# Preparing the first two units of a feed-forward on VectorE and ScalarE instead of GpSimd

## Chip, cores and metric

The kernel runs on one core of a Trainium2 chip. The metric is the device time of one execution in microseconds (us), the median of three runs. A time within a trace is given in us from the start of its span.

## What is computed

One inference step of a decoder layer for 1,088 tokens (1,024 of a prompt, 64 of samples) with a model width of 1,024: feed-forward a, a mixer (a state-space scan beside sparse attention), an attention over memory, feed-forward b, a final norm. The change touches both feed-forwards and nothing else. Each of them is, in float32:

```python
def rmsnorm(x, g):
    xf = x.astype(jnp.float32)
    xf = xf * lax.rsqrt(jnp.mean(xf * xf, axis=-1, keepdims=True) + EPS)
    return (xf * g.astype(jnp.float32)).astype(x.dtype)

def swiglu_ffn(x, g, w_in, w_out):
    h = rmsnorm(x, g) @ w_in
    gate, up = jnp.split(h, 2, axis=-1)
    return (jax.nn.silu(gate) * up) @ w_out        # D_FF = 2816
```

## The kernel before

`ffn_stage` is called twice, at the program's start ("first feed-forward") and at its end ("second", from 2093.7 us). Its product of x with the gate and up weights is done as 2x2 blocks with seven products instead of eight (M1 to M7): five are of a sum or difference of blocks on one side or both. A float32 factor is split in two parts, high (ScalarE rounds it, `round_w` L555 and `round_h` L573) and low (VectorE subtracts the high part, `rest_w` L820 and `rest_h` L815), and each product is three matmuls (L674 to L676).

A unit is one tile of gate and up outputs by one half of the tokens; there are 44. For the first two units, u = 0 and 1, the operands of x must first be made. That goes in eight blocks j = 0 to 7 (`PREPS`), four for each unit: block j is 272 columns by two pairs of the 128-row tiles of x. For a block:

- `scale(j)`, VectorE, L807 to L809: x times the norm's weights, two instructions of 128x272 and one of 128x544. It also fills one of two buffers `b12`, and waits until block j - 2 has been turned.
- `turn(j)`, GpSimd, L513 to L518: four differences T1 to T4 of 128x272. T2 needs T1, and T4 needs T2.
- `round_h(j)`, ScalarE, then `rest_h(j)`, VectorE: both parts of all seven operands, one instruction of 128x1904 each.
- TensorE: seven products, 21 matmuls of 272 columns.
- In the first feed-forward alone also `square(j)` on ScalarE (L566, two of 128x544) and 16 matmuls of 136 columns (L687), which sum the squares for the norm. The second has them from the stage before it.

The weights of the first tile arrive as four blocks. `combine(0)`, GpSimd, L525 to L533, makes five sums of 128x512, each from parts that `rest_w` has let go of (the order is fixed by the semaphores `w_ready` and `s_made`). Later tiles have their sums made on VectorE already, in its own `combine(f, n)`.

After block 3, `first_unit(0)` (L851 to L866) adds the products of unit 0 on VectorE. In the first feed-forward a ScalarE root (`root`, L580, with a table load) must come before three of these adds and before the fourth block's TensorE products from M2 on. After block 7 comes `invert(0)` (L901, a reciprocal of 3.55 us), then the gate of unit 0, `first_unit(1)`, and from `invert(1)` on the loop over units 2 to 43. Every engine works its list in the written order:

```python
                scale(0)
                scale(1)
                for a in (A11, A12):
                    rest_w(0, a)
                rest_h(0)
                for a in (S1, S3, S2, S4, A22):
                    rest_w(0, a)
                for j in range(1, PREPS):
                    if j + 1 < PREPS:
                        scale(j + 1)
                    rest_h(j)
```

## Time and profile before

| | |
|---|---|
| median of 3 runs | 2914.68 us (2910.53 to 2921.82) |
| the profiled execution, its own time | 2912.39 us |
| its span | 2910.7 us |
| TensorE busy | 2671.4 us, 92% |
| VectorE, ScalarE, GpSimd busy | 1589.0, 986.7, 222.8 us |
| first feed-forward, 0 to 80 us: TensorE, VectorE, GpSimd busy | 46.87, 55.84, 45.57 us |
| second, 2115 to 2170 us: TensorE, VectorE, GpSimd busy | 33.22, 45.14, 28.28 us |

The profiled execution lies 2.3 us under the median of the runs. Busy time says who works; the chain of waits and the timelines say who is waited for. Two instructions of one engine overlap a little in the records, so that the distance between two starts, not the duration of one, is what an instruction costs in a queue.

### The profile page before, as it was taken

How to read it: one execution, taken by the hardware profiler on the slowest of the kernel's cores; microseconds unless marked ns; L12 is line 12 of the kernel's file. 1: busy time of each engine (PE TensorE's matmuls, PEld its weight loads, DVE VectorE, ACT ScalarE, POOL GpSimd, SP SyncE). 2: the span in 40 equal slices, each digit the busy share in tenths (PEclk: the TensorE clock that was granted, in tenths of full speed). 3: DMA queues.
4: the chain of work that ended last, by engine and by line, in shares of the span. 5: the costliest groups of instructions: out<-in, count | busy, mean ns of one | idle time of the engine just before them, and what ended most of it. 6: DMA issues, size and time to landing. Idle time of an engine off the chain costs nothing. (4 is left out here: it accounts for less than half of the span.)

```text
span 2910.7 us, 47240 instructions
## 1 busy us (share of the span) xinstructions
PE 2671.4 (92%) x18982; PEld 2506.4 (86%) x18982; DVE 1589.0 (55%) x2870; ACT 986.7 (34%) x2080; POOL 222.8 (8%) x248
## 2 busy tenths in 40 slices
PE   6899999999979998999589997797769999999998
PEld 5899999999969997898467774697669999999997
DVE  6766666544264111343477663565586666665434
ACT  4333333311144222221266662343433333332111
POOL 6000000000000000110200004030440000000000
PEclk9999999999989998998699997798879999999999
DMA  2222222512035324130300005203012222232121
GB/s 96 71 85 69 78 79 71 191 75 75 1 137 107 40 75 168 39 99 5 101 23 23 8 1 190 119 11 104 16 37 78 79 71 86 68 132 107 75 75 62
DMA packets 121995, 220.29 MB, mean 76 GB/s; under 512 B 12834, under 2 KB 76754, under 8 KB 120242
## 3 DMA queue, kind: packets, MB, share of 16 engines
q1 hardware_dynamic: 115922, 201.51, 21.6%
q10 hardware_dynamic: 2880, 9.07, 0.8%
q0 software_dynamic: 2976, 6.68, 0.7%
q8 instruction: 152, 2.49, 0.4%
q14 instruction: 65, 0.53, 0.1%
HBM read 170.80 MB, written 48.24 MB: 75 GB/s over the span
## 5 line engine op out<-in xcount | busy, mean ns | idle before, releaser
L674 PE MATMUL ffn_gate_up<-ffn_h_hi,ffn_w 128*128 128x272 f32 x1912 | 560.0, 293 | 60.7 <-DVE ffn_h_lo L815 42.6
L675 PE MATMUL ffn_gate_up<-ffn_h_lo,ffn_w 128*128 128x272 f32 x1912 | 557.5, 292 | 0.0
L676 PE MATMUL ffn_gate_up<-ffn_h_hi,ffn_w 128*128 128x272 f32 x1912 | 556.7, 291 | 0.0
L674 PEld LDWEIGHTS ffn_gate_up<-ffn_h_hi,ffn_w 128*128 128x128 f32 x1912 | 364.8, 191 | 66.2 <-DVE ffn_h_lo L815 32.5
L676 PEld LDWEIGHTS ffn_gate_up<-ffn_h_hi,ffn_w 128*128 128x128 f32 x1912 | 364.7, 191 | 0.0
L675 PEld LDWEIGHTS ffn_gate_up<-ffn_h_lo,ffn_w 128*128 128x128 f32 x1912 | 364.6, 191 | 0.0
L1007 DVE SCALAR_TENSOR_TENSOR x<-ffn_down,x 128x364 f32<-128x364 f32 (+1 forms) x240 | 126.3, 534 | 327.7 <-PE ffn_down L235 327.7
L820 DVE TENSOR_TENSOR ffn_w<-ffn_w_raw,ffn_w 128x512 fp32r<-128x512 f32 x264 | 187.8, 714 | 102.7 <-ACT ffn_w L555 102.7
L555 ACT ACTIVATE ffn_w<-ffn_w_raw 128x512 fp32r<-128x512 f32 x264 | 159.9, 624 | 97.3 <-PE ffn_down L676 79.1
L674 PE MATMUL ffn_down<-ffn_h_hi,ffn_w 128*128 128x272 f32 x552 | 163.6, 296 | 13.4 <-DVE ffn_w L820 7.9
L233 PE MATMUL mix_ps<-h_mix_hi,mix_w_hi 128*128 128x364 f32 x480 | 161.0, 335 | 9.3 <-issue 6.1
L675 PE MATMUL ffn_down<-ffn_h_lo,ffn_w 128*128 128x272 f32 x552 | 162.1, 294 | 0.0
L676 PE MATMUL ffn_down<-ffn_h_hi,ffn_w 128*128 128x272 f32 x552 | 161.9, 293 | 0.0
L234 PE MATMUL mix_ps<-h_mix_lo,mix_w_hi 128*128 128x364 f32 x480 | 160.0, 333 | 0.0
L235 PE MATMUL mix_ps<-h_mix_hi,mix_w_lo 128*128 128x364 f32 x480 | 159.8, 333 | 0.0
L1929 DVE TENSOR_TENSOR mix_w_lo<-mix_w_raw,mix_w_hi 128x1024 fp32r<-128x1024 f32 (+1 forms) x26 | 32.1, 1233 | 196.5 <-ACT mix_w_hi L1814 196.5
L1295 PE MATMUL ssd_hid_ps<-ssd_pages,ssd_cmp_w 128*128 128x128 f32 (+1 forms) x1024 | 138.8, 294 | 0.0
L2394 DVE TENSOR_REDUCE pn_neg_max<-pn_s_ps 128x1 f32<-128x640 f32 (+7 forms) x128 | 90.4, 707 | 88.2 <-PE pn_s_ps L2221 49.1
L1295 PEld LDWEIGHTS ssd_hid_ps<-ssd_pages,ssd_cmp_w 128*128 128x128 f32 x1024 | 131.7, 193 | 2.4
L651 ACT ACTIVATE ffn_h_hi<-ffn_h_raw 128x1088 fp32r<-128x1088 f32 x44 | 48.7, 1107 | 232.1 <-DMA ffn_h_raw<-scratch_ffn_act 232.0
L586 ACT ACTIVATE ffn_sums<-ffn_sums 128x544 f32<-128x544 f32 x88 | 58.0, 659 | 201.9 <-DVE ffn_sums L873 201.8
L233 PE MATMUL ffn_down<-ffn_h_hi 128*128 128x364 f32 (+1 forms) x384 | 126.2, 329 | 0.0
(520 smaller groups left out, 6506.2 us busy)
## 6 DMA issues: line engine op xcount, KB each, us to landing
ffn_w_raw<-in_w_ffn_in SPq DMA_DIRECT2D x88, 512.0 KB, 3.9
scratch_ffn_act<-ffn_prod SPq DMA_DIRECT2D x88, 272.0 KB, 2.6
ffn_h_raw<-scratch_ffn_act SPq DMA_DIRECT2D x44, 544.0 KB, 7.0
mix_w_raw<-in_w_mix SPq DMA_DIRECT2D x20, 512.0 KB, 3.5
ffn_h_raw<-in_w_ffn_out SPq DMA_DIRECT2D x16, 512.0 KB, 9.2
ssd_pages<-in_cmp_pages SPq DMA_DIRECT2D x64, 128.0 KB, 2.1
ffn_w_sum<-in_w_ffn_out SPq DMA_DIRECT2D x14, 512.0 KB, 11.1
scratch_x<-x SPq DMA_DIRECT2D x1, 4368.0 KB, 16.7
```

Of the source, the lines that this page charges most:

```text
L233: pe.matmul(out, w_hi, x_hi, start=start, stop=False)
L234: pe.matmul(out, w_hi, x_lo, start=False, stop=False)
L235: return pe.matmul(out, w_lo, x_hi, start=False, stop=stop)
L555: act.activation(w[:, a, 0, :], fresh(a), ACT.Copy).then_inc(w_hi_ready, 1)
L586: act.activation(gate_view(u), gate_view(u), ACT.Silu).then_inc(gate_done, 1)
L674: pe.matmul(out, hi, x_hi, start=start, stop=False, skip_group_check=chained)
L675: pe.matmul(out, hi, x_lo, start=False, stop=False, skip_group_check=chained)
L676: mm = pe.matmul(out, lo, x_hi, start=False, stop=stop, skip_group_check=chained)
L820: dve.tensor_tensor(w[:, a, 1, :], fresh(a), w[:, a, 0, :].bitcast(F32), ALU.subtract).then_inc(w_ready, 1)
L1007: dve.scalar_tensor_tensor(xT[:, t, cols], dn_bank(d), 0.5, xT[:, t, cols], ALU.mult, ALU.add).then_inc(dn_added, 1)
L1295: mm = pe.matmul(hp[j % 2][:, 1 - later:1 - later + w].rearrange("p (b n) -> p b n", n=PAGES), w1s[:, kv, k, hh * P:(hh + 1) * P], pages[: ...
L2394: m = dve.tensor_reduce(neg_max[:, u % 2, 0:1], s[:, 0:w], AX_X, ALU.max, negate=True)
```

## The change

GpSimd keeps only a memset. Its `turn` goes to VectorE for all eight blocks, and so does its `combine(0)`, now interleaved one by one with the `rest_w` of the first tile. `scale(j)` stays on VectorE for j = 0 and 1 and goes to ScalarE for j = 2 to 7 (`OWN_SCALES = 2`), as three copies with a scale read from memory. ScalarE rounds block 0 before all weights, and `square(j)` comes one block later in its queue. The load of the norm's weights is put ahead of the first block of x.

```diff
--- before.py
+++ after.py
@@ -265,6 +265,7 @@
 UPPER_BANKS_FIRST = ("M5", "M6", "M7", "M1", "M2", "M4", "M3")
 WIDTHS = (TG, TG, HALVES * HALF - 2 * TG)
 DOWN_CHUNKS = (2, 5, 5, 5, 5)
+OWN_SCALES = 2
 
 
 def in_two_types(nc, stack, name, shape):
@@ -502,42 +503,11 @@
                 if fin is not None:
                     fin.stores(sp)
 
-            @block.gpsimd
-            def _(pool):
-                def turn(j):
...
-                    pool.wait_ge(scaled_x, j + 1)
-                    pool.tensor_tensor(at_(T1), extra, at_(B11), ALU.subtract).then_inc(turned, 1)
...
-                def combine(f):
...
-                if first_loads is not None:
                     pool.memset(xT[:, :, HALVES * HALF:], 0.0).then_inc(pads_ready, 1)
-                turn(0)
-                combine(0)
-                for j in range(1, PREPS):
-                    turn(j)
+            if first_loads is not None:
+                @block.gpsimd
+                def _(pool):
+
             def fresh(a):
 
                 return {A11: raw[:, 0], A12: raw[:, 1], S2: w_raw[:, S2, 1, :], S1: raw[:, 2], S3: raw[:, 0],
@@ -565,6 +535,19 @@
                             act.wait_ge(sq_summed, j)
                         act.activation(out, x_block(xT, j)[:, n], ACT.Square).then_inc(sq_ready, 1)
 
+                def scale(j):
+
+                    g, kp = divmod(j, K_PAIRS)
+                    if arrivals is not None:
+                        act.wait_ge(arrivals[j], 32)
+                    act.wait_ge(turned, 4 * max(j - 1, OWN_SCALES))
+                    src = x_block(xT, j)
+                    by = lambda k: gain[:, k:k + 1]
+                    act.activation(b12[:, j % 2, :], src[:, 0, 1, :], ACT.Copy, scale=by(kp))
+                    act.activation(h_raw[:, g, B11, kp, :], src[:, 0, 0, :], ACT.Copy, scale=by(kp))
+                    act.activation(h_raw[:, g, B21:B22 + 1, kp, :], src[:, 1, :, :], ACT.Copy, scale=by(kp + K_PAIRS)
+                                   ).then_inc(scaled_x, 1)
+
                 def round_h(j):
                     g, kp = divmod(j, K_PAIRS)
                     act.wait_ge(turned, 4 * (j + 1))
@@ -595,20 +578,22 @@
                                        bias=core.eps[:, 0:1]).then_inc(rms_ready, 1)
                 else:
                     square(0)
-                for a in (A11, A12):
+                round_h(0)
+                for a in (A11, A12, S1, S3, S2, S4, A22):
                     round_w(0, a)
-                round_h(0)
-                for a in (S1, S3, S2, S4, A22):
-                    round_w(0, a)
+                scale(OWN_SCALES)
                 for j in range(1, PREPS):
                     round_h(j)
+                    if not summed_before and j >= 2:
+                        square(j - 1)
+                    if j + OWN_SCALES < PREPS:
+                        scale(j + OWN_SCALES)
                     if j == K_PAIRS:
                         first_copy(0)
                         if not summed_before:
                             root(0)
-                    if not summed_before:
-                        square(j)
                 if not summed_before:
+                    square(PREPS - 1)
                     root(1)
                 first_copy(1)
                 for a in (A11, A12):
@@ -800,8 +785,6 @@
                         dve.wait_ge(arrivals[j], 32)
                         if j == 0:
                             dve.wait_ge(gain_landed, 16)
-                    if j >= 2:
-                        dve.wait_ge(turned, 4 * (j - 1))
                     src = x_block(xT, j)
                     by = lambda k: gain[:, k:k + 1]
                     dve.tensor_scalar(h_raw[:, g, B11, kp, :], src[:, 0, 0, :], by(kp), None, ALU.mult)
@@ -809,6 +792,19 @@
                     dve.tensor_scalar(h_raw[:, g, B21:B22 + 1, kp, :], src[:, 1, :, :], by(kp + K_PAIRS), None, ALU.mult
                                       ).then_inc(scaled_x, 1)
 
+                def turn(j):
+
+                    g, kp = divmod(j, K_PAIRS)
+                    at_ = lambda op: h_raw[:, g, op, kp, :]
+                    extra = b12[:, j % 2, :]
+                    dve.wait_ge(scaled_x, j + 1)
+                    dve.tensor_tensor(at_(T1), extra, at_(B11), ALU.subtract).then_inc(turned, 1)
+                    dve.tensor_tensor(at_(T3), at_(B22), extra, ALU.subtract).then_inc(turned, 1)
+                    dve.wait_ge(turned, 4 * j + 1)
+                    dve.tensor_tensor(at_(T2), at_(B22), at_(T1), ALU.subtract).then_inc(turned, 1)
+                    dve.wait_ge(turned, 4 * j + 3)
+                    dve.tensor_tensor(at_(T4), at_(B21), at_(T2), ALU.subtract).then_inc(turned, 1)
+
                 def rest_h(j):
                     g, kp = divmod(j, K_PAIRS)
                     dve.wait_ge(h_hi_ready, j + 1)
@@ -824,6 +820,7 @@
 
                     done = (N - 2) * f
                     if n == 0:
+                        dve.wait_ge(up_landed, 16 * (f + 1))
                         dve.wait_ge(w_ready, N * f + 1)
                         dve.tensor_tensor(raw[:, 0], raw[:, 0], raw[:, 2], ALU.subtract).then_inc(s_made, 1)
                     elif n == 1:
@@ -837,7 +834,8 @@
                         dve.wait_ge(s_made, done + 3)
                         dve.tensor_tensor(raw[:, 1], raw[:, 1], raw[:, 0], ALU.add).then_inc(s_made, 1)
                     else:
-                        dve.wait_ge(m_ready, made_at[2 * f - 1, READ_BY[S2]])
+                        if f:
+                            dve.wait_ge(m_ready, made_at[2 * f - 1, READ_BY[S2]])
                         dve.tensor_tensor(w_raw[:, S2, 1, :], raw[:, 3], raw[:, 0], ALU.subtract).then_inc(s_made, 1)
 
                 def first_unit(u, between):
@@ -908,15 +906,28 @@
                                       ).then_inc(c12_done, 1)
 
                 scale(0)
-                scale(1)
-                for a in (A11, A12):
-                    rest_w(0, a)
+                turn(0)
+                if arrivals is None:
+                    scale(1)
+                    turn(1)
                 rest_h(0)
-                for a in (S1, S3, S2, S4, A22):
+                rest_w(0, A11)
+                combine(0, 0)
+                rest_w(0, A12)
+                for n in (1, 2):
+                    combine(0, n)
+                rest_w(0, S1)
+                combine(0, 3)
+                rest_w(0, S3)
+                combine(0, 4)
+                if arrivals is not None:
+                    scale(1)
+                    turn(1)
+                for a in (S2, S4, A22):
                     rest_w(0, a)
                 for j in range(1, PREPS):
                     if j + 1 < PREPS:
-                        scale(j + 1)
+                        turn(j + 1)
                     rest_h(j)
                     if j == K_PAIRS:
                         first_unit(0, lambda: None)
@@ -3578,11 +3589,11 @@
 
         def first_loads(sp, load_weights):
 
+            sp.dma_start(gains[:], i["gains"]).then_inc(gains_landed, 16)
             for j in range(PREPS):
                 for half in range(2):
                     sp.dma_start(x_block(x, j)[:, half], x_block(i["x"], j)[:, half]).then_inc(x_landed[j], 16)
                 if j == 0:
-                    sp.dma_start(gains[:], i["gains"]).then_inc(gains_landed, 16)
                     load_weights()
             sp.dma_start(inner_gains[:], i["inner_gains"]).then_inc(rest_landed, 16)
             sp.dma_start(core.all_consts[:], i["consts"]).then_inc(rest_landed, 16)
```

How instructions move, as the built program lists them (names: `ffn_h_raw` the operands of x before the split, `ffn_b_78` the buffer `b12`, `ffn_w_raw` and `ffn_w_sum` the weights and their sums). VectorE, first feed-forward, from block 0's scale to the first weights, before:

```order
L807 TENSOR_SCALAR ffn_h_raw<-x,gains 128x272
L808 TENSOR_SCALAR ffn_b_78<-x,gains 128x272
L809 TENSOR_SCALAR ffn_h_raw<-x,gains 128x2x272
L807 TENSOR_SCALAR ffn_h_raw<-x,gains 128x272
L808 TENSOR_SCALAR ffn_b_78<-x,gains 128x272
L809 TENSOR_SCALAR ffn_h_raw<-x,gains 128x2x272
L820 TENSOR_TENSOR ffn_w<-ffn_w_raw,ffn_w 128x512 x2
L815 TENSOR_TENSOR ffn_h_lo<-ffn_h_raw,ffn_h_hi 128x7x272
L820 TENSOR_TENSOR ffn_w<-ffn_w_raw,ffn_w 128x512 x2
```

and now:

```order
L790 TENSOR_SCALAR ffn_h_raw<-x,gains 128x272
L791 TENSOR_SCALAR ffn_b_78<-x,gains 128x272
L792 TENSOR_SCALAR ffn_h_raw<-x,gains 128x2x272
L801 TENSOR_TENSOR ffn_h_raw<-ffn_b_78,ffn_h_raw 128x272
L802 TENSOR_TENSOR ffn_h_raw<-ffn_h_raw,ffn_b_78 128x272
L804 TENSOR_TENSOR ffn_h_raw<-ffn_h_raw 128x272
L806 TENSOR_TENSOR ffn_h_raw<-ffn_h_raw 128x272
L811 TENSOR_TENSOR ffn_h_lo<-ffn_h_raw,ffn_h_hi 128x7x272
L816 TENSOR_TENSOR ffn_w<-ffn_w_raw,ffn_w 128x512
L825 TENSOR_TENSOR ffn_w_raw<-ffn_w_raw 128x512
L816 TENSOR_TENSOR ffn_w<-ffn_w_raw,ffn_w 128x512
L829 TENSOR_TENSOR ffn_w_raw<-ffn_w_raw 128x512
```

The second `scale` has moved back, behind the weight sums; four differences and the sums of GpSimd stand among the subtractions of the weights.

VectorE in the steady part, blocks 2 and 3, before:

```order
L807 TENSOR_SCALAR ffn_h_raw<-x,gains 128x272
L808 TENSOR_SCALAR ffn_b_78<-x,gains 128x272
L809 TENSOR_SCALAR ffn_h_raw<-x,gains 128x2x272
L815 TENSOR_TENSOR ffn_h_lo<-ffn_h_raw,ffn_h_hi 128x7x272
L807 TENSOR_SCALAR ffn_h_raw<-x,gains 128x272
L808 TENSOR_SCALAR ffn_b_78<-x,gains 128x272
L809 TENSOR_SCALAR ffn_h_raw<-x,gains 128x2x272
L815 TENSOR_TENSOR ffn_h_lo<-ffn_h_raw,ffn_h_hi 128x7x272
```

and now:

```order
L801 TENSOR_TENSOR ffn_h_raw<-ffn_b_78,ffn_h_raw 128x272
L802 TENSOR_TENSOR ffn_h_raw<-ffn_h_raw,ffn_b_78 128x272
L804 TENSOR_TENSOR ffn_h_raw<-ffn_h_raw 128x272
L806 TENSOR_TENSOR ffn_h_raw<-ffn_h_raw 128x272
L811 TENSOR_TENSOR ffn_h_lo<-ffn_h_raw,ffn_h_hi 128x7x272
L801 TENSOR_TENSOR ffn_h_raw<-ffn_b_78,ffn_h_raw 128x272
L802 TENSOR_TENSOR ffn_h_raw<-ffn_h_raw,ffn_b_78 128x272
L804 TENSOR_TENSOR ffn_h_raw<-ffn_h_raw 128x272
L806 TENSOR_TENSOR ffn_h_raw<-ffn_h_raw 128x272
L811 TENSOR_TENSOR ffn_h_lo<-ffn_h_raw,ffn_h_hi 128x7x272
```

Three multiplications are gone and four differences have come, ahead of each `ffn_h_lo`. ScalarE in the same part, before:

```order
L573 ACTIVATE ffn_h_hi<-ffn_h_raw 128x7x272
L566 ACTIVATE ffn_h_squares<-x 128x2x272 x2
L573 ACTIVATE ffn_h_hi<-ffn_h_raw 128x7x272
L566 ACTIVATE ffn_h_squares<-x 128x2x272 x2
```

and now:

```order
L548 ACTIVATE ffn_h_raw<-x,gains 128x2x272
L556 ACTIVATE ffn_h_hi<-ffn_h_raw 128x7x272
L536 ACTIVATE ffn_h_squares<-x 128x2x272 x2
L546 ACTIVATE ffn_b_78<-x,gains 128x272
L547 ACTIVATE ffn_h_raw<-x,gains 128x272
L548 ACTIVATE ffn_h_raw<-x,gains 128x2x272
L556 ACTIVATE ffn_h_hi<-ffn_h_raw 128x7x272
```

Each block now has three multiplications more on ScalarE, between its squares and the rounding of the next block.

## Rows read from the trace of the kernel before

**Rows 1.** The chain that ended last, 2085 to 2175 us: start us, length us, what

```profile
2114.87 2.61 POOL ffn_h_raw L514
```

**Rows 2.** Waits of TensorE, 0:80, then 2090:2175 us: us in total, times, longest

```profile
PE ffn_gate_up L674 <- DVE ffn_h_lo L815: 20.7, 5, 15.2
...
PE ffn_gate_up L674 <- DVE ffn_h_lo L815: 21.9, 5, 11.8
```

**Rows 3.** Timeline of VectorE, second feed-forward: start us, length us, idle before it in brackets

```profile
2093.78 0.36 DVE L807 TENSOR_SCALAR ffn_h_raw<-x,gains 128x272 f32<-128x272 f32 x1 [2.83 <-PEq L53]
...
2120.97 2.74 DVE L815 TENSOR_TENSOR ffn_h_lo<-ffn_h_raw,ffn_h_hi 128x1904 fp32r<-128x1904 f32 x1 [1.56 <-ACT ffn_h_hi L573]
...
2134.29 0.42 DVE L851 TENSOR_TENSOR ffn_v<-ffn_sums,ffn_down 128x272 f32<-128x272 f32 x1
...
2149.81 2.14 DVE L815 TENSOR_TENSOR ffn_h_lo<-ffn_h_raw,ffn_h_hi 128x1904 fp32r<-128x1904 f32 x1 [2.48 <-ACT ffn_h_hi L573]
2151.87 3.55 DVE L901 RECIPROCAL ffn_inv<-ffn_inv 128x544 f32<-128x544 f32 x1
...
2167.72 3.55 DVE L901 RECIPROCAL ffn_inv<-ffn_inv 128x544 f32<-128x544 f32 x1
```

**Rows 4.** Timeline of GpSimd, second feed-forward

```profile
2119.49 0.77 POOL L513 TENSOR_TENSOR ffn_h_raw<-ffn_b,ffn_h_raw 128x272 f32<-128x272 f32 x1 [0.38 <-DVE ffn_h_raw L809]
```

**Rows 5.** Timeline of VectorE, first feed-forward

```profile
5.40 0.36 DVE L807 TENSOR_SCALAR ffn_h_raw<-x,gains 128x272 f32<-128x272 f32 x1 [4.10 <-DMA gains<-in_gains]
...
5.95 0.50 DVE L809 TENSOR_SCALAR ffn_h_raw<-x,gains 128x544 f32<-128x544 f32 x1
...
47.80 0.42 DVE L851 TENSOR_TENSOR ffn_v<-ffn_sums,ffn_down 128x272 f32<-128x272 f32 x1
...
65.78 3.55 DVE L901 RECIPROCAL ffn_inv<-ffn_inv 128x544 f32<-128x544 f32 x1
...
75.99 0.69 DVE L835 TENSOR_TENSOR ffn_w_raw<-ffn_w_raw 128x512 f32<-128x512 f32 x1
...
77.35 0.44 DVE L892 TENSOR_TENSOR ffn_prod<-ffn_sums,ffn_prod 128x272 f32<-128x272 f32 x1
...
81.25 0.69 DVE L820 TENSOR_TENSOR ffn_w<-ffn_w_sum,ffn_w 128x512 fp32r<-128x512 f32 x1 [0.69 <-ACT ffn_w L555]
...
82.21 3.54 DVE L901 RECIPROCAL ffn_inv<-ffn_inv 128x544 f32<-128x544 f32 x1
```

**Rows 6.** Timeline of ScalarE, first feed-forward

```profile
49.17 1.20 ACT L566 ACTIVATE ffn_h_squares<-x 128x544 f32<-128x544 f32 x2
50.26 1.79 ACT L573 ACTIVATE ffn_h_hi<-ffn_h_raw 128x1904 fp32r<-128x1904 f32 x1
...
81.12 0.61 ACT L555 ACTIVATE ffn_w<-ffn_w_raw 128x512 fp32r<-128x512 f32 x1
```

**Rows 7.** Line 580 on ScalarE, all its instructions

```profile
L580 ACT ACTIVATE ffn_inv<-ffn_gate_up,const_eps x4: 480/486/490, 48.4 to 68.4; 128x272 f32<-128x272 f32 x4
L580 ACT ACT_TABLE_LOAD  x1: 1283/1283/1283, 47.1 to 47.1; - x1
```

**Rows 8.** TensorE, the sixteen square sums of a block at the faster pace

```profile
33.16 2.02 PE L687 MATMUL ffn_gate_up<-ffn_h_squares,const_mean_model 128*128 128x136 f32 x16
```

**Rows 9.** Timeline of TensorE, second feed-forward: two pairs of neighbours

```profile
2117.77 0.43 PE L674 MATMUL ffn_gate_up<-ffn_h_hi,ffn_w 128*128 128x272 f32 x1
2118.00 0.43 PE L675 MATMUL ffn_gate_up<-ffn_h_lo,ffn_w 128*128 128x272 f32 x1
...
2141.22 0.29 PE L676 MATMUL ffn_down<-ffn_h_hi,ffn_w 128*128 128x272 f32 x1
2141.35 0.29 PE L674 MATMUL ffn_down<-ffn_h_hi,ffn_w 128*128 128x272 f32 x1
```

**Rows 10.** Windows of TensorE: us, busy (count), granted clock, DMA share, GB/s

```profile
2115.00:2120.00 5.00, 3.07 (x13) 0.50 0.22 80
2140.00:2145.00 5.00, 2.92 (x21) 1.00 0.00 0
```

More of the change, by code:

```diff
@@ L503, in _ @@
                     fin.stores(sp)
-            @block.gpsimd
-            def _(pool):
-                def turn(j):
-                    g, kp = divmod(j, K_PAIRS)
-                    at_ = lambda op: h_raw[:, g, op, kp, :]
-                    extra = b12[:, j % 2, :]
-                    pool.wait_ge(scaled_x, j + 1)
-                    pool.tensor_tensor(at_(T1), extra, at_(B11), ALU.subtract).then_inc(turned, 1)
-                    pool.tensor_tensor(at_(T3), at_(B22), extra, ALU.subtract).then_inc(turned, 1)
-                    pool.wait_ge(turned, 4 * j + 1)
-                    pool.tensor_tensor(at_(T2), at_(B22), at_(T1), ALU.subtract).then_inc(turned, 1)
-                    pool.wait_ge(turned, 4 * j + 3)
-                    pool.tensor_tensor(at_(T4), at_(B21), at_(T2), ALU.subtract).then_inc(turned, 1)
-                def combine(f):
-                    done = (N - 2) * f
-                    pool.wait_ge(up_landed, 16 * (f + 1))
-                    pool.wait_ge(w_ready, N * f + 1)
-                    pool.tensor_tensor(raw[:, 0], raw[:, 0], raw[:, 2], ALU.subtract).then_inc(s_made, 1)
-                    pool.wait_ge(s_made, done + 1)
-                    pool.wait_ge(up_rest_landed, 16 * (f + 1))
-                    pool.tensor_tensor(raw[:, 2], raw[:, 2], raw[:, 3], ALU.add).then_inc(s_made, 1)
-                    pool.wait_ge(w_ready, N * f + 2)
-                    pool.tensor_tensor(raw[:, 1], raw[:, 1], raw[:, 3], ALU.subtract).then_inc(s_made, 1)
-                    pool.wait_ge(s_made, done + 3)
-                    pool.tensor_tensor(raw[:, 1], raw[:, 1], raw[:, 0], ALU.add).then_inc(s_made, 1)
-                    pool.tensor_tensor(w_raw[:, S2, 1, :], raw[:, 3], raw[:, 0], ALU.subtract).then_inc(s_made, 1)
-                if first_loads is not None:
+            if first_loads is not None:
+                @block.gpsimd
+                def _(pool):
                     pool.memset(xT[:, :, HALVES * HALF:], 0.0).then_inc(pads_ready, 1)
-                turn(0)
-                combine(0)
-                for j in range(1, PREPS):
-                    turn(j)
             def fresh(a):
```

## Prediction

> **What bounds the kernel now.** Over the whole span TensorE is busy 92%, so a gain can only come from where it waits. I looked for such places in the parts that the change touches, at the head of the two feed-forwards. The chain of waits shows there one piece of work after another on GpSimd, the longest of 2.61 us for a difference of 272 columns [rows 1]. The waits of TensorE say whom it waits for: VectorE's `rest_h`, 20.7 us in the first feed-forward (15.2 of them the wait for its first matmul) and 21.9 us in the second (11.8 the first) [rows 2]. In the timeline of VectorE the reader is to see why that is late: `rest_h` L815 sits idle for ScalarE (1.56 us, 2.48 us), which has waited for GpSimd's last difference, and it takes 2.74 us beside GpSimd and 2.14 us without it [rows 3]. GpSimd shows the same: 0.77 us for a difference that runs undisturbed [rows 4] and 2.61 us for one that doesn't [rows 1]. The Trainium skill says of this ("SBUF — State Buffer", section on its two separate sides) that VectorE with two SBUF inputs and GpSimd exclude each other from a shared port for a whole instruction. By that rule the stretching ends with GpSimd's part, and it speaks against the rival on ScalarE contention below.
>
> So the pair VectorE and GpSimd bounds the preparation. The marks that I count to are VectorE's first add of unit 0 (L851, at 47.80 and 2134.29), the first reciprocal (65.78 and 2151.87) and the second (82.21 and 2167.72) [rows 3, 5]. From the second reciprocal on, the loop over units runs as before, so what is gained there stays gained.
>
> **Prices.** A multiplication of 272 columns costs VectorE 0.28 us in its queue (two from 5.40 to 5.95), one of 544 columns takes 0.50; two-input work from SBUF takes 0.44 at 272 columns (L892) and 0.69 at 512 (L835) [rows 5]. Neighbours overlap by 0.08 (2149.81 + 2.14 against 2151.87 [rows 3]). Thus on VectorE: `scale` 1.05 to its result; `turn` 0.36 + 0.36 + 0.44 + 0.05 for the hand-over before T4 + 0.36 = 1.57; a sum or a `rest_w` 0.61; `rest_h` 2.06. ScalarE: `square` 1.1, `round_h` 1.79 (1.70 in the queue) [rows 6]. A multiplication there reads its factor from memory, as L580 reads its bias: 0.49 at 272 columns [rows 7]; two of these and one of 544 (0.74, a square's 0.64 of a pair of 1.20 plus the 0.1 that the bias costs) make `scale` 1.4. The chip has not shown this instruction here: its bounds are 1.1 (the rows without such an operand) and 2.8 (twice), and I take 1.4, the row with the nearest form. TensorE: 21 matmuls at 0.13 = 2.7 us at the upper clock level (2.4 GHz), at 0.23 = 4.8 us at the lower (1.2 GHz), and 16 for squares 2.0 us [rows 8 to 10].
>
> **Per block.** VectorE pays 1.57 + 2.06 = 3.63 us, ScalarE 1.4 + 1.7 = 3.1, and 4.2 with squares. TensorE pays 2.7, and with squares 4.7. Before, from 2120.97 to 2149.81 five blocks pass, 5.8 us each with the adds of unit 0 among them [rows 3]. So the second feed-forward becomes bound by VectorE at 3.63, the first by TensorE at 4.7.
>
> **Second feed-forward.** VectorE starts at 2093.78 [rows 3]. Two `scale` 1.9, two `turn` 3.1 and hand-overs 0.3 bring `rest_h(0)` to 2099.1; its rounding on ScalarE is done by then. Then 2.06, and twelve of 0.61 (seven `rest_w`, five sums) = 7.3, and 1.1 of waits (the last sum S2 goes to ScalarE and back with no cover, 0.7): 2109.6. The rounding of block 1 stands behind ScalarE's last weights and `scale(2)`, 0.7 late. Four blocks of 3.63: `rest_h(4)` ends at 2124.8, L851 starts at 2124.8, against 2134.29. The adds take 2.7 as before; two blocks and a `rest_h` 9.3: reciprocal at **2136.8** against 2151.87. The distance between the two reciprocals, 15.85, has neither GpSimd nor moved work in it. Gain **15.1 us**.
>
> **First feed-forward.** The weights of the norm no longer arrive last, but x comes one issue later: start at 5.6 against 5.40 [rows 5], 0.2 lost. Scale 1.05, turn 1.65, rounding 1.8, `rest_h` 2.1, `rest_w` 0.7: TensorE starts at 13.1 against 15.2 [rows 2]. VectorE's list goes on: 7.3 for the twelve, 0.4 of waits, `scale(1)` and `turn(1)` 2.6 (they cover S2's way over ScalarE), to 22.7, then 3.63: `rest_h(1)` ends at 26.3. Now TensorE: three blocks at 4.7, 0.5 for a start at the lower clock level, less the last three products (1.1), plus 0.6 for the last squares: L851 at 40.4 against 47.80. Then the root: table load 1.28 and two of 0.49 [rows 7], behind which TensorE's block 4 waits. It goes on at 43.6, ends blocks 4 and 5 at 52.8; `round_h(7)` waits for block 5's squares, 1.8 + 2.2 with its `rest_h`: reciprocal at **57.1** against 65.78. Behind it 16.4 as before, plus 0.5: TensorE ends the products of block 7 that the next weights wait for at 60.6, with copy and rounding 61.7, and VectorE is free at 61.2. Second reciprocal at 74.0, gain **8.2 us**.
>
> **Sum.** 15.1 + 8.2 = 23.3 us. VectorE's added work, (8 x 1.57 + 5 x 0.61 - 6 x 0.97) = 9.8 us per feed-forward, is inside these chains. 2912.4 of the profiled execution becomes 2889.1; its median lies 2.3 higher, so 2891.4.
>
> **Rivals.** *ScalarE becomes the bound* (7%). With `scale` at 2.8 a block costs it 4.5 and 5.6 us, 0.9 above both limits: over six blocks 5.4 in each, 12.5 us gained in all, 2902. Against it: L580's duration. *TensorE stays at the lower level* (5%). In the first feed-forward a block then takes 4.8 + 2.7 = 7.5 us against 6 before, 8 us lost; the second still gains 9 at 4.8: 2913.5. For it: 0.50 between 2115 and 2120 [rows 10]. Against it: shorter pauses. The Trainium skill ("TensorE: Matmul & The Clock Gate", what is actually happening) has the lower level as the default, which activity lifts; the trace agrees, 0.50 with 3.07 us busy of 5 and 1.00 later [rows 10]. *The differences cost VectorE what they cost GpSimd* (5%), 0.77: `turn` 2.9, a block 5.0, gain 4: 2911. *Slower* (3%): ScalarE beside VectorE stretches each of its instructions as GpSimd does. At 0.5 us each a block has 5 x 0.5 more, 6.1 us, above TensorE's limit, and twelve weights' instructions 6 more: some 15 us lost in each feed-forward, 2945. It decides from 0.35 us each on, in proportion. Against it: `rest_w` at 81.25 takes 0.69 [rows 5] while ScalarE works from 81.12 to 81.73 [rows 6].
>
> **How the numbers follow.** The forecast has 80%, with 2882 to 2899 as its own range (hand-overs of 0.12 instead of 0.05 cost 4 us, the runs before scatter by -4 and +7). The range of 8 in 10 reaches to ScalarE's rival: 2881 to 2904. A measurement here tells about 0.5%, 14.6 us, from no change. Faster by more: the forecast and a little of ScalarE's rival, 0.82. Within 0.5%: the rest of it, the clock, the dear differences, 0.14. Slower: 0.04.
>
> **What would show it.** No GpSimd in the preparation; VectorE's `rest_h` at 2.14 throughout, every 3.6 us in the second feed-forward; 128x272 differences of 0.44; ScalarE's multiplications of 0.49; reciprocals near 57 and 74 in the first, 43 and 59 us after its start in the second. It would be wrong if the multiplications take 0.8, if `rest_h` waits for ScalarE in every block, or if TensorE runs at 0.23 per matmul into unit 1.

## The result, and the profile after

The changed kernel takes 2890.53 us (median of 4 runs, 2889.35 to 2891.76), the kernel before 2914.81 (median of 4, 2910.53 to 2921.82): a ratio of 0.9912, with a 95% interval of 0.9898 to 0.9925. That is **faster**, by 0.9%, with an interval that excludes no change; by the medians 24.3 us where 23.3 were forecast. The profiled execution took 2890.69 us, its span is 2889.0.

The first lines of the profile's page for the changed kernel: TensorE's busy time fell by 2.3 us against the table ahead, VectorE's by 3.7, ScalarE's rose by 16.8, and GpSimd's fell by 90.8.

```profile
span 2889.0 us, 47283 instructions
...
PE 2669.1 (92%) x18982; PEld 2503.6 (87%) x18982; DVE 1585.3 (55%) x2908; ACT 1003.5 (35%) x2116; POOL 132.0 (5%) x174
```

VectorE took on 16 `turn` and 10 sums and is yet busy for less: it gave away 12 `scale`, and its remaining work is no longer stretched. The timeline of VectorE in the second feed-forward answers to [rows 3]:

```profile
2086.61 0.36 DVE L790 TENSOR_SCALAR ffn_h_raw<-x,gains 128x272 f32<-128x272 f32 x1 [2.83 <-PEq L53]
...
2102.98 0.44 DVE L801 TENSOR_TENSOR ffn_h_raw<-ffn_b,ffn_h_raw 128x272 f32<-128x272 f32 x1 [0.61 <-ACT ffn_h_raw L548]
...
2104.66 2.14 DVE L811 TENSOR_TENSOR ffn_h_lo<-ffn_h_raw,ffn_h_hi 128x1904 fp32r<-128x1904 f32 x1
...
2108.26 2.13 DVE L811 TENSOR_TENSOR ffn_h_lo<-ffn_h_raw,ffn_h_hi 128x1904 fp32r<-128x1904 f32 x1
...
2117.48 0.43 DVE L849 TENSOR_TENSOR ffn_v<-ffn_sums,ffn_down 128x272 f32<-128x272 f32 x1
...
2129.38 3.54 DVE L899 RECIPROCAL ffn_inv<-ffn_inv 128x544 f32<-128x544 f32 x1
...
2145.30 3.55 DVE L899 RECIPROCAL ffn_inv<-ffn_inv 128x544 f32<-128x544 f32 x1
```

L811 is `rest_h`, L801 the first difference of `turn`, L849 the first add of unit 0 (L851 before) and L899 the reciprocal (L901 before). `rest_h` takes 2.13 or 2.14 each time, starts every 3.6 us from block 1 to block 4, and never waits for ScalarE. Up to the first reciprocal VectorE stands idle three times: for the program's stage before (2.83), for ScalarE's rounding of the last weight sum (0.70), and for ScalarE's first `scale` (0.61).

The first feed-forward, to be read beside [rows 5]:

```profile
5.62 0.36 DVE L790 TENSOR_SCALAR ffn_h_raw<-x,gains 128x272 f32<-128x272 f32 x1 [4.32 <-DMA x<-in_x]
...
27.70 2.13 DVE L811 TENSOR_TENSOR ffn_h_lo<-ffn_h_raw,ffn_h_hi 128x1904 fp32r<-128x1904 f32 x1
...
31.50 2.14 DVE L811 TENSOR_TENSOR ffn_h_lo<-ffn_h_raw,ffn_h_hi 128x1904 fp32r<-128x1904 f32 x1
...
34.06 0.44 DVE L801 TENSOR_TENSOR ffn_h_raw<-ffn_b,ffn_h_raw 128x272 f32<-128x272 f32 x1 [0.42 <-ACT ffn_h_raw L548]
...
39.40 0.44 DVE L849 TENSOR_TENSOR ffn_v<-ffn_sums,ffn_down 128x272 f32<-128x272 f32 x1 [1.51 <-ACT ffn_sums L573]
...
53.92 2.14 DVE L811 TENSOR_TENSOR ffn_h_lo<-ffn_h_raw,ffn_h_hi 128x1904 fp32r<-128x1904 f32 x1 [3.17 <-ACT ffn_h_hi L556]
...
55.98 3.54 DVE L899 RECIPROCAL ffn_inv<-ffn_inv 128x544 f32<-128x544 f32 x1
...
72.82 3.54 DVE L899 RECIPROCAL ffn_inv<-ffn_inv 128x544 f32<-128x544 f32 x1
```

Here VectorE is no longer the bound from block 3 on: it waits for ScalarE's `scale` (0.42), for the copy of the first product (1.51), and for a rounding behind TensorE's squares (3.17). The waits of TensorE from 0 to 72 us, and below them those from 2080 to 2155, answer to [rows 2]:

```profile
PE ffn_gate_up L659 <- DVE ffn_w L816: 14.0, 3, 13.1
PE ffn_gate_up L659 <- DVE ffn_h_lo L811: 0.5, 1, 0.5
...
PE ffn_gate_up L659 <- DVE ffn_w L816: 15.3, 4, 9.4
PE ffn_gate_up L659 <- DVE ffn_h_lo L811: 5.8, 2, 3.2
```

Waits for `rest_h` of 20.7 and 21.9 us have become 0.5 and 5.8, but a part of that is only a change of name: TensorE's first matmul now needs a `rest_w` last, and its wait stands with the weights. That first wait went from 15.2 to 13.1 us and from 11.8 to 9.4; the waits for `rest_h` behind it went from 5.5 to 0.5 and from 10.1 to 5.8.

Where the time went, by the starts on VectorE (those of the second feed-forward counted from its first `scale`):

| kernel | 1st: adds | reciprocals | 2nd: adds | reciprocals |
|---|---|---|---|---|
| before | 47.80 | 65.78, 82.21 | +40.51 | +58.09, +73.94 |
| changed | 39.40 | 55.98, 72.82 | +30.87 | +42.77, +58.69 |

The first head gained 82.21 - 72.82 = 9.4 us, the second 73.94 - 58.69 = 15.2, together 24.6. The span fell by 21.7 only. The experiments ask which part brought what, what sets the first head's pace now, and where the missing 2.9 us are.

### The profile page after: what moved, and what is told of

Read it like the earlier page. It is cut to its first block and busy times, and to the rows that moved or that the text cites. A ratio compares the mean times of both kernels' runs of the same rounds, so it can differ in the third digit from the quotient of the medians.

```text
span 2889.0 us, 47283 instructions
## 1 busy us (share of the span) xinstructions
PE 2669.1 (92%) x18982; PEld 2503.6 (87%) x18982; DVE 1585.3 (55%) x2908; ACT 1003.5 (35%) x2116; POOL 132.0 (5%) x174
## 5 line engine op out<-in xcount | busy, mean ns | idle before, releaser
L816 DVE TENSOR_TENSOR ffn_w<-ffn_w_raw,ffn_w 128x512 fp32r<-128x512 f32 x264 | 181.1, 687 | 96.9 <-ACT ffn_w L525 96.7
```

The source lines that it names most:

```text
L816: dve.tensor_tensor(w[:, a, 1, :], fresh(a), w[:, a, 0, :].bitcast(F32), ALU.subtract).then_inc(w_ready, 1)
```

## The experiments

All edits are to the changed kernel. Marks are the second reciprocal of each feed-forward, against 72.82 and +58.69. Ratios are to the kernel before, run beside the experiment. The change itself has 0.9898 to 0.9925, so an experiment whose interval overlaps that is not told from the change by its time on the whole, and the marks have to speak.

### Each part undone by itself

**VectorE keeps all multiplications.** ScalarE's `scale` calls go, and VectorE's list gets them back:

```diff
                     if j + 1 < PREPS:
+                        if j:
+                            scale(j + 1)
                         turn(j + 1)
```

> The change with one part undone: all eight multiplications of x by the norm's weights on VectorE, the differences and sums stay there too. Theory (VectorE bounds the second feed-forward, TensorE the first): VectorE pays 6 x 0.97 = 5.8 us more in each. In the second, from its first instruction to the second reciprocal, 58.7 us become about 63.8 (5.8 less the 0.6 that VectorE waited for ScalarE). In the first a block costs VectorE 4.6, just under TensorE's 4.7: its second reciprocal moves from 72.8 to about 74.5. Sum: 6 to 7 us slower than the change, 2897. Rival (ScalarE's share was of no use, the gain is GpSimd's absence alone): within 1 us of the change, 2890 to 2892.

Measured: 2899.95 us, ratio to before 0.9939 (0.9918 to 0.9961). Marks 75.33 and +64.29: 2.5 and 5.6 us late. VectorE in the second feed-forward, two blocks:

```profile
2104.22 2.13 DVE L810 TENSOR_TENSOR ffn_h_lo<-ffn_h_raw,ffn_h_hi 128x1904 fp32r<-128x1904 f32 x1
...
2108.88 2.13 DVE L810 TENSOR_TENSOR ffn_h_lo<-ffn_h_raw,ffn_h_hi 128x1904 fp32r<-128x1904 f32 x1
```

A block now takes 4.66 (2104.22 to 2108.88) against 3.60: `scale` costs 1.06 where the prediction had 1.05. Six of it, less the 0.61 of waiting that it replaces, are 5.8, near the 5.6 us, so VectorE bounds the second head and every microsecond of its list shows. In the first head only part shows, as another engine bounds it there.

**The differences back on GpSimd.** `turn` moves as it stands:

```diff
+            @block.gpsimd
+            def _(pool):
+                def turn(j):
...
+                    pool.tensor_tensor(at_(T1), extra, at_(B11), ALU.subtract).then_inc(turned, 1)
...
+                for j in range(PREPS):
+                    turn(j)
```

> The change with the differences T1 to T4 of all blocks back on GpSimd; sums on VectorE, multiplications on ScalarE as changed. Theory (the two engines shut each other out): 272-column differences of 0.77 us that reach 2.5 beside rest_h, rest_h 2.1 to 2.7; a block costs 5 us or more and the chain difference, rounding, rest_h lies open. Second feed-forward 58.7 us become 66 to 70, the first's second reciprocal 72.8 becomes 77 to 81; 2903 to 2910. Rival (only the queue on GpSimd behind the five sums was slow): with the sums gone GpSimd has time for 3.1 us per block, under VectorE's 2.1 to 3.6, and the time stays within 3 us of the change.

Measured: 2906.78 us, ratio 0.9968 (0.9950 to 0.9987). Marks 79.81 and +66.92: 7.0 and 8.2 late, the dearest part of the change to miss. GpSimd in the second feed-forward, from one block's first difference to the next block's:

```profile
2117.75 0.77 POOL L514 TENSOR_TENSOR ffn_h_raw<-ffn_b,ffn_h_raw 128x272 f32<-128x272 f32 x1
...
2120.05 2.55 POOL L519 TENSOR_TENSOR ffn_h_raw<-ffn_h_raw 128x272 f32<-128x272 f32 x1
2122.56 0.77 POOL L514 TENSOR_TENSOR ffn_h_raw<-ffn_b,ffn_h_raw 128x272 f32<-128x272 f32 x1
```

and VectorE beside it:

```profile
2119.64 2.32 DVE L813 TENSOR_TENSOR ffn_h_lo<-ffn_h_raw,ffn_h_hi 128x1904 fp32r<-128x1904 f32 x1 [2.47 <-ACT ffn_h_hi L571]
2124.46 2.32 DVE L813 TENSOR_TENSOR ffn_h_lo<-ffn_h_raw,ffn_h_hi 128x1904 fp32r<-128x1904 f32 x1 [2.49 <-ACT ffn_h_hi L571]
```

Three differences take 0.77 or 0.76, the fourth 2.55, as it lies under a `rest_h` (2119.64 to 2121.96). The block becomes 4.82, and VectorE idles half of it. GpSimd has no gap (2117.75 to 2122.56), so it sets this pace. With all four at 0.77 the block would be some 3.0, an estimate from these rows (4.81 less 1.78) and less than VectorE's 3.60: by this estimate it is the meeting of the two engines, more than GpSimd's own speed, that makes the differences dear there.

**The sums of weights back on GpSimd.**

```diff
-                combine(0, 0)
...
+                for a in (S1, S3, S2, S4, A22):
```

> The change with the five sums of the first weights back on GpSimd, differences on VectorE. Theory: the chain of the sums takes 1.27 each undisturbed and up to 3 beside VectorE, against 0.61; block 0's last weights come 2 to 4 us later (first feed-forward: from 22.5 to 25 to 26 us; second: from 15.8 us after its start to 18 to 20). That goes into the second feed-forward in full and into the first in part, for TensorE waits for these weights there: 4 to 6 us slower than the change, 2895 to 2897. Rival (sums are hidden behind TensorE's first block): within 1 us.

Measured: 2896.60 us, ratio 0.9927 (0.9904 to 0.9949). Marks 74.85 and +61.12: 2.0 and 2.4 late. GpSimd's sums:

```profile
2099.54 1.59 POOL L513 TENSOR_TENSOR ffn_w_raw<-ffn_w_raw 128x512 f32<-128x512 f32 x1 [25.50 <-DVE ffn_w L832]
2101.20 1.26 POOL L516 TENSOR_TENSOR ffn_w_raw<-ffn_w_raw 128x512 f32<-128x512 f32 x1
```

A sum costs GpSimd 1.26 and more, VectorE 0.61. It took five such instructions off VectorE (3.05 us), and was late all the same.

The marks of the three parts add up to 8.1 + 15.2 + 4.5 = 27.8 us for undoing each alone, against 24.6 for the whole: some 3 us are won only where two parts stand together, and are counted twice here. The new order on ScalarE (block 0 rounded before all weights, the squares one block later) was not undone by itself; its share stays open.

**The gains' load behind x's first block.**

```diff
-            sp.dma_start(gains[:], i["gains"]).then_inc(gains_landed, 16)
             for j in range(PREPS):
...
                 if j == 0:
+                    sp.dma_start(gains[:], i["gains"]).then_inc(gains_landed, 16)
                     load_weights()
```

> The change with the load of the norm's weights put back behind the first block of x. Theory: a start at 5.40 again instead of 5.62, so 0.2 us earlier at the second reciprocal of the first feed-forward (72.8 to 72.6); nothing in the second. Rival (it was needed): the weights land last and the start moves later than 5.62.

Measured in one execution: 2891.95 us, marks 73.42 and +58.68. VectorE's first line:

```profile
6.15 0.36 DVE L790 TENSOR_SCALAR ffn_h_raw<-x,gains 128x272 f32<-128x272 f32 x1 [4.85 <-DMA gains<-in_gains]
```

It starts at 6.15 instead of 5.62, waiting for the gains and not for x. The theory's 0.2 us were not gained. The DMA issues of the first 10 us show the small load slow here:

```profile
gains<-in_gains SPq DMA_DIRECT2D x1, 24.0 KB, 3.4
```

In the kernel before, with the same order, it took 2.7 us and VectorE started at 5.40 [rows 5]; ahead of x it takes 1.8. So the order is worth between -0.2 and +0.5 us by these traces, and single traces scatter as widely with the order of the change: 5.86 for the changed kernel in a later trace, and 6.15, waiting for x, in the kernel with half the sums below. What the order is worth is not told from nothing.

### What the moved work meets

**ScalarE multiplies each block twice.** The three multiplications are issued a second time, with a wait between the two sets.

```diff
+                    act.activation(b12[:, j % 2, :], src[:, 0, 1, :], ACT.Copy, scale=by(kp)).then_inc(once, 1)
...
+                    act.wait_ge(once, 3 * (j - OWN_SCALES) + 3)
                     act.activation(b12[:, j % 2, :], src[:, 0, 1, :], ACT.Copy, scale=by(kp))
```

> The change with ScalarE's three multiplications of a block done twice, the second time behind a wait for the first: 1.4 us more per block on ScalarE and nothing else. It is the ScalarE rival of the prediction made real. Theory: a block costs ScalarE 4.6 (second feed-forward) and 5.7 us (first), over VectorE's 3.6 and TensorE's 4.7, so 0.9 us are lost for each of six blocks in both: second reciprocal at 72.8 + 5 and the second feed-forward 58.7 + 5.5; 10 us slower than the change, 2901. Rival (ScalarE has slack of 1 us per block and more, and the differences are made ahead): under 3 us.

Measured: 2909.22 us, ratio 0.9964 (0.9951 to 0.9977). Marks 81.38 and +65.07: 8.6 and 6.4 late, 15 in all where 10 were expected. VectorE in the first feed-forward:

```profile
34.77 0.44 DVE L807 TENSOR_TENSOR ffn_h_raw<-ffn_b,ffn_h_raw 128x272 f32<-128x272 f32 x1 [2.02 <-ACT ffn_h_raw L554]
...
36.46 2.14 DVE L817 TENSOR_TENSOR ffn_h_lo<-ffn_h_raw,ffn_h_hi 128x1904 fp32r<-128x1904 f32 x1
...
42.30 2.14 DVE L817 TENSOR_TENSOR ffn_h_lo<-ffn_h_raw,ffn_h_hi 128x1904 fp32r<-128x1904 f32 x1
```

A block takes 5.84 (36.46 to 42.30) and 4.75 in the second feed-forward, and each waits for ScalarE. The pace without the edit is 4.5 and 3.6, so six blocks lose 1.3 and 1.15 each, where the prediction's rival had 0.9 for a `scale` of 2.8. The reason lies in the edit. ScalarE's first set, the first instruction of the second set, and the rounding behind it:

```profile
31.57 0.51 ACT L547 ACTIVATE ffn_b<-x,gains 128x272 f32<-128x272 f32 x1
...
33.16 0.52 ACT L552 ACTIVATE ffn_b<-x,gains 128x272 f32<-128x272 f32 x1
...
34.64 1.78 ACT L562 ACTIVATE ffn_h_hi<-ffn_h_raw 128x1904 fp32r<-128x1904 f32 x1
```

With the wait between its sets `scale` takes 3.07 (31.57 to 34.64), 0.27 more than the rival's 2.8. Twelve blocks of that are 3.2 us; without them the loss would be some 11.8, an estimate, near the 10.8 of the rival. So the rival was priced about right, and its condition (a dearer `scale`) did not come.

**GpSimd kept busy beside VectorE.** Eight subtractions of 272 columns run on GpSimd, on buffers that are free then, from block 1's differences on; VectorE's first adds wait for the last of them.

```diff
+                pool.wait_ge(turned, 8)
+                for n in range(8):
+                    pool.tensor_tensor(u22[:], prod[:, 0, :], prod[:, 1, :], ALU.subtract).then_inc(busy_done, 1)
+                    pool.wait_ge(busy_done, n + 2)
```

> The change with eight subtractions of 128x272 added on GpSimd, on buffers that nobody needs then, from block 1's differences on; VectorE waits for them only before its adds of unit 0, when they are long done. Theory (one shuts the other out of SBUF for a whole instruction): GpSimd's take 0.77 alone and up to 2.6 beside rest_h, VectorE's rest_h 2.13 grows to 2.3 to 2.9 and its differences 0.44 to 0.9; in the second feed-forward, which VectorE bounds, 4 to 6 us are lost before the adds (30.9 becomes 35 to 37), in the first less, 1 to 4. Rival (GpSimd was slow only because its work lay in the chain): VectorE's durations stay, nothing is lost.

Measured in one execution: 2904.55 us, marks 76.72 and +63.16: 3.9 and 4.5 late. GpSimd, and VectorE at the same time:

```profile
2101.93 10.73 POOL L515 TENSOR_TENSOR ffn_u<-ffn_prod 128x272 f32<-128x272 f32 x8 [5.25 <-DVE ffn_h_raw L813]
```

```profile
2108.43 1.25 DVE L839 TENSOR_TENSOR ffn_w_raw<-ffn_w_raw 128x512 f32<-128x512 f32 x1
2109.61 1.25 DVE L823 TENSOR_TENSOR ffn_w<-ffn_w_raw,ffn_w 128x512 fp32r<-128x512 f32 x1
2110.78 1.25 DVE L842 TENSOR_TENSOR ffn_w_raw<-ffn_w_raw 128x512 f32<-128x512 f32 x1
```

VectorE's two-input instructions of 512 columns start 1.17 apart, where they start 0.61 apart alone; GpSimd's eight take 10.73 together: the first, under a `rest_h`, 2.52, and the other seven start 1.17 apart like VectorE's, where its differences start 0.73 apart while VectorE idles. So VectorE's 0.61 and what one GpSimd instruction adds make the 1.17, and both engines keep the same pace: they work as if by turns. The Trainium skill ("SBUF — State Buffer", section on its two separate sides) says that they exclude each other for a whole instruction; the distances agree. No such stretching is seen from ScalarE, which worked beside VectorE throughout.

### What sets the pace of the first head

**Half the sums of squares left out.** Of the two steps of four matmuls that sum a block's squares (sixteen records in the profile), TensorE leaves out the first, so that this half of the squares is missing from the norm.

```diff
-                        for b in range(4):
+                        for b in range(4 if n else 0):
```

> The change with 8 instead of 16 matmuls for the squares of a block (the norm is then of half the rows: this part of the computation is left out). Theory (TensorE bounds the first feed-forward): 1.0 us less per block on TensorE, 4.7 becomes 3.7, about VectorE's 3.6; from block 1 to block 7 some 5 us: first reciprocal 56.0 becomes 51, second 72.8 becomes 67.5. Rival (VectorE or ScalarE bounds it, TensorE's squares fit beside): under 1 us. The second feed-forward keeps 58.7.

Measured in one execution: 2896.77 us, marks 72.61 and +58.69, first reciprocal 56.02 against 55.98. The forecast 5 us were not gained. It started 0.5 us later, by x's landing, so from there 0.5 us were gained. TensorE's timeline shows what happened next. The changed kernel:

```profile
23.59 2.69 PE L672 MATMUL ffn_gate_up<-ffn_h_squares,const_mean_model 128*128 128x136 f32 x16
26.31 0.40 PE L659 MATMUL ffn_gate_up<-ffn_h_hi,ffn_w 128*128 128x272 f32 x1
26.54 0.29 PE L660 MATMUL ffn_gate_up<-ffn_h_lo,ffn_w 128*128 128x272 f32 x1
...
30.84 0.38 PE L659 MATMUL ffn_gate_up<-ffn_h_hi,ffn_w 128*128 128x272 f32 x1
...
35.35 0.38 PE L659 MATMUL ffn_down<-ffn_h_hi,ffn_w 128*128 128x272 f32 x1
```

The kernel with half the sums:

```profile
24.13 2.02 PE L672 MATMUL ffn_gate_up<-ffn_h_squares,const_mean_model 128*128 128x136 f32 x8
26.85 0.59 PE L659 MATMUL ffn_gate_up<-ffn_h_hi,ffn_w 128*128 128x272 f32 x1 [0.71 <-DVE ffn_h_lo L811]
...
31.32 0.29 PE L660 MATMUL ffn_gate_up<-ffn_h_lo,ffn_w 128*128 128x272 f32 x1
...
38.35 1.17 PE L672 MATMUL ffn_gate_up<-ffn_h_squares,const_mean_model 128*128 128x136 f32 x8 [0.99 <-ACT ffn_h_squares L536]
```

With fewer squares TensorE waited 0.71 for block 1, and then ran that whole block with matmuls 0.23 apart (the lower level) up to 31.3, where the changed kernel had 0.13 (the upper) from 26.5 on: 19 or so matmuls at 0.1 more gave back 1.9 us. The late start is not what kept it there: the kernel with the gains behind x starts at 6.15 too, and its matmuls are 0.13 apart from 27.1 on. Whether it was the fewer matmuls or the pause of 0.71 is not shown. And later TensorE waited 0.99 for ScalarE's squares. Two things were mixed here, so the next one takes the first away.

**Late squares halved.** The same, but only from the third block on (`range(4 if n or j < 2 else 0)`), again with that part of the squares missing from the norm.

> The change, but TensorE leaves out the first four of the eight matmuls in each step of the squares from the third block on (that part of x's squares is missing from the norm); in the first two blocks nothing is left out, so TensorE is at its upper level from the second block on as in the changed kernel. It takes 1.0 us from each of the steps at 33.58 and 36.55. Theory A (TensorE alone sets the first feed-forward's blocks): the adds 2.0 us earlier, at 37.4, and the first reciprocal 2 us earlier or more. Theory B (ScalarE, whose rounding, squares and scales take 4.24 per block, sets them just behind TensorE's 4.5): the adds at most 0.6 earlier, at 38.8, as ScalarE comes to its copy at 38.4 whatever TensorE does, and TensorE waits for squares instead. The second feed-forward is unchanged (+30.9, +42.8, +58.7), as it has no such steps.

Measured in one execution: 2888.30 us, adds at 39.11 against 39.40, reciprocals 54.75 and 71.33. The adds moved by 0.3 us, not 2.0: theory B. ScalarE's timeline there:

```profile
35.78 1.19 ACT L536 ACTIVATE ffn_h_squares<-x 128x544 f32<-128x544 f32 x2
...
37.70 0.73 ACT L548 ACTIVATE ffn_h_raw<-x,gains 128x544 f32<-128x544 f32 x1
38.69 0.40 ACT L573 ACTIVATE ffn_sums<-ffn_gate_up 128x272 f32<-128x272 f32 x1 [0.26 <-PE ffn_gate_up L661]
```

Up to 38.4 it works without a gap, and TensorE, a step ahead, waits 0.99 for its squares (at 37.11): TensorE's gain turned into waits. Thus TensorE (4.5 per block) and ScalarE (4.24) bound the first head together. Behind the adds, in the blocks of unit 1, the 1.2 us of the first reciprocal do come through, where the last rounding waits for the squares' sums.

**The roots' table early.** Two kernels load the table of ScalarE's square root before x has landed; the first also brings the first weight's rounding and first sum ahead of `rest_h(0)`.

```diff
                 else:
+                    act.activation(inv[:, 0:1], core.eps[:, 0:1], ACT.Sqrt)
                     square(0)
+                    round_w(0, A11)
```

> The change with two edits in the first feed-forward: a one-column root as ScalarE's first instruction, so that the table of the root is loaded before the data arrive and not before the first root; and the first weight block rounded before block 0 of x, with its low part and the first sum made in VectorE's wait. Theory: the load of 1.28 us is in TensorE's way before block 4 and goes, VectorE's list is 1 us shorter behind block 0: second reciprocal of the first feed-forward 72.8 becomes about 71, the second feed-forward keeps 58.7; 2 us faster than the change, 2888.5. Rival (squares and roots are hidden behind TensorE's own work): 72.8 stays.

> The change, with one added one-column square root as ScalarE's first work of the first feed-forward, so that the table that the roots need (1.28 us at 40.13 in the changed kernel) is loaded while x is still on its way; nothing else. Theory (the load lies on the path from the sums of the squares to the first reciprocal): in the first feed-forward the adds start as in the changed kernel (39.40), the roots 1.3 earlier, both reciprocals 1.2 earlier (54.8 and 71.6); the second feed-forward is unchanged; the whole 1 us under the changed kernel, which is less than the runs can tell, so the trace decides. Rival (the early run with the weights gained by its other part): reciprocals at 55.98 and 72.82 as in the changed kernel.

Measured: 2889.49 us, ratio 0.9897 (0.9881 to 0.9914), marks 71.61 and +58.68; and, with the table alone, 2888.74, ratio 0.9904 (0.9890 to 0.9918), marks 71.59 and +58.67. ScalarE with the table alone:

```profile
1.59 1.28 ACT L580 ACT_TABLE_LOAD   x1 [1.59 <-PEq L1081]
...
5.68 1.20 ACT L536 ACTIVATE ffn_h_squares<-x 128x544 f32<-128x544 f32 x2 [2.59 <-DMA x<-in_x]
```

The roots start at 40.21 instead of 41.43, and both reciprocals are 1.2 us earlier. All of it is the table; the weight part gained nothing. The first weight comes to ScalarE at 9.28 only, and the rounding of block 0 behind it starts at 9.82, against 8.35 in the changed kernel:

```profile
9.28 0.63 ACT L525 ACTIVATE ffn_w<-ffn_w_raw 128x512 fp32r<-128x512 f32 x1 [2.37 <-DMA ffn_w_raw<-in_w_ffn_in]
```

So TensorE starts at 13.82 instead of 13.13, and what VectorE's shorter list gains behind it makes up for that. Over the whole kernel 1.2 us can't be told from none (the interval of the unaltered kernel, below, overlaps); it is shown on the marks alone.

### Where the missing 2.9 us are

**The changed kernel once more**, without an edit.

> The changed kernel itself, in the same rounds as the kernel with the early table and beside the kernel before. Theory (the 2.2 us that are given back between the first reciprocals and the second feed-forward depend on when TensorE pauses, not on moved work): the marks inside both feed-forwards repeat to 0.1 us from their starts (39.4, 56.0, 72.8; +30.9, +42.8, +58.7), while the distance from the second reciprocal of the first to the start of the second may differ from the 2013.8 of the first trace by a few us. Rival (fixed by the order of work): 2013.8 again within 0.2 us. Ratio to the kernel before 0.990 to 0.993 in either case.

Measured: 2889.95 us, ratio 0.9918 (0.9905 to 0.9931). One of its six executions took 9118.62 us, for a reason that nothing here shows; without it the median is 2889.55. The marks repeat: 56.22 and 73.06, +42.76 and +58.66. The way between the two heads does not:

| kernel | from the second reciprocal to the second head's first `scale` | span |
|---|---|---|
| before | 2011.6 | 2910.7 |
| changed | 2013.8 | 2889.0 |
| changed, once more | 2008.6 | 2883.5 |
| table early | 2015.1 | 2889.4 |
| VectorE keeps `scale` | 2010.6 | 2895.0 |

The same program passes the same work in 2008.6 and in 2013.8 us, and the difference of 5.2 is nearly all of the 5.5 between its two spans. The missing 2.9 us are 2.2 here (2011.6 to 2013.8) and 0.7 behind the second head. Both lie within what one execution differs from the next, so nothing in the traces makes them an effect of the change; the kernel before has one trace only. Over all thirteen traces of this case the distance runs from 2008.6 to 2019.7, the latter in the kernel with half the sums, which is why its 2896.77 on the whole is so far behind its marks. Between the two traces of the changed kernel the difference comes in steps over the stages between: on VectorE equal within 0.3 up to 825 us, then on TensorE up to 3 us later and up to 5 earlier. What sets it in one execution stays open.

## Why the prediction was right

| step of the prediction | forecast | measured |
|---|---|---|
| ScalarE's `scale` | 1.4 (bounds 1.1, 2.8) | 1.48: 20.82 to 22.30, parts 0.52, 0.51, 0.73 |
| VectorE's block in the second head | 3.63 | 3.60 |
| second head: adds | +31.0 | +30.87 |
| second head: reciprocals | +43.0, +58.9 | +42.77, +58.69 |
| first head: start, TensorE's start | 5.6, 13.1 | 5.62, 13.06 |
| first head: end of `rest_h(1)` | 26.3 | 26.2 |
| TensorE's block in the first head | 4.7 | 4.5: 26.31, 30.84, 35.35 |
| first head: a start at the lower clock level | 0.5 | none: 0.13 apart from 26.54 on |
| first head: adds | 40.4 | 39.40 |
| first head: reciprocals | 57.1, 74.0 | 55.98, 72.82 |
| gains | 15.1 + 8.2 | 15.2 + 9.4 |

*The second head* came out by every step. VectorE bounds it, as the kernel that gives it the multiplications back shows: its block grew by 1.06, and the mark by 5.6.

*The first head* gained 1.2 us more than forecast, 1.0 of it up to the adds. From TensorE's block 1 to the adds the sum had 14.1 us, and it took 13.1 (26.31 to 39.40). Two terms were mis-sized by some 0.5 each. One is TensorE's step of squares: I took its recorded 2.02 us [rows 8]; what it costs in the queue is 1.77 (29.07 to 30.84), the next matmul starting before its modelled end, and so the three blocks took 4.53, 4.51 and 4.05 where the sum has 4.7, 4.7 and 4.2. The other is the start at the lower clock level, which did not come: the matmuls are 0.13 apart from 26.54 on. Two sums also do not add up as written: TensorE's start comes to 12.9 by its terms where 13.1 stands, and the first reciprocal to 56.8 where 57.1 stands; 0.5 us have no name there.

*"The first by TensorE"* was only half right. ScalarE follows at 4.24 per block without a gap, and a TensorE made 2 us lighter gained 0.3 at the adds. The forecast held because both limits lie close together.

*"What is gained there stays gained"* holds on the average: the medians differ by 24.3 and, beside the later runs, 2914.98 - 2889.95 = 25.0, against 24.6 gained in the two heads. In one pair of traces it can be off by several microseconds either way. So it is partly luck that the median came within 1 us of the forecast 2891.4; the marks, which were 1.3 us better than forecast, are the firmer check.

*The rivals.* ScalarE as a bound did not come, as its multiplication with a factor from memory costs 0.51, near L580's 0.49 [rows 7]; doubling it showed a loss of 15 us, some 11.8 by estimate at the rival's own 2.8, where the rival priced 10.8. TensorE at the lower level did not come in the first head's later blocks, but one experiment came near: with half the sums, after a pause of 0.71 us at 26, it was there for another 4.5 us. The differences at GpSimd's price did not come either: 0.44. The slower rival, ScalarE stretching VectorE, is refuted by L811's 2.13 throughout while ScalarE was busy for 5.00 of 5 us from 25 to 30; what does stretch VectorE is GpSimd.

## What to carry to other kernels

Where VectorE and GpSimd work on SBUF at once, price it as taking turns, and ask what each instruction costs when alone. In the kernel that keeps all multiplications on VectorE, that engine does all its old work and all of GpSimd's, and is busy for 1596.8 us against 1589.0 before: work of some 31 us by the prediction's prices, an estimate, added 7.8. Price a step by the distance between starts, not by the recorded duration, since the error grows with each block. And before a few microseconds missing from a span are explained, run the same program twice: here the marks inside a stage repeat to 0.3 us, while the way through the rest differs by 5, and over all traces by 11.

## What the runs showed of the hardware that was not expected

- GpSimd's 272-column difference took 0.77 us alone (0.72 between starts), 1.17 between starts beside VectorE's 512-column instructions, and 2.55 beside one long `rest_h`; VectorE's 512-column instruction went from 0.61 to 1.17 between starts.
- VectorE's multiplications, with one large input from SBUF, are stretched too. In the kernel before, the one below lies under a difference of GpSimd (2126.71 to 2129.38) and takes 0.86, against 0.36 alone:

```profile
2128.67 0.86 DVE L807 TENSOR_SCALAR ffn_h_raw<-x,gains 128x272 f32<-128x272 f32 x1
```

- At the start of a trace the row of granted clocks does not tell TensorE's level. Up to 65 us it shows 1.00 in the kernels before, changed and with half the sums, although the changed kernel's 272-column matmuls start 0.23 apart up to 23.6 us and those of the kernel with half the sums up to 31.3. Later the row follows (0.50 with 0.23 apart [rows 9, 10]). Here the distance between starts tells. The row for the kernel with half the sums:

```profile
25.00:30.00 5.00, 4.29 (x20) 3.97 (x19) 4.96 (x6) 5.00 (x9) 0.00 (x0) 1.00 0.23 80
```
